# Gated delta rule of a two-block model: the chunk inverse in 64x64 products, value rows scaled by ScalarE, modulation steps placed elsewhere

## The chip, the cores and the metric

The kernel runs on one core of a Trainium2 chip. The metric is the device time of one execution in microseconds; of the kernel before there are three runs. The profile shows one more execution with its own time.

## The reference, cut to what matters

The program computes two transformer-like blocks over 256 tokens of width 2048. The part around the change is the gated delta rule of the first block: 8 heads, key and value width 128, chunks of 64 tokens in the reference. Each chunk solves a unit lower triangular system.

```python
def gated_delta_chunked(q, k, v, log_a, beta):
    qc, kc, vc = to_chunks(q), to_chunks(k), to_chunks(v)
    g = jnp.cumsum(...); bc = to_chunks(beta)
    gamma = jnp.exp(jnp.where(incl, g[..., :, None] - g[..., None, :], -jnp.inf))
    kk = jnp.einsum('nbhtk,nbhsk->nbhts', kc, kc)
    m = jnp.where(strict, bc[..., :, None] * kk * gamma, 0.0)
    a_mat = jnp.eye(CHUNK) + m
    rhs = jnp.concatenate([vc * bc[..., None], kc * (bc * jnp.exp(g))[..., None]], axis=-1)
    sol = lax.linalg.triangular_solve(a_mat, rhs, left_side=True, lower=True, unit_diagonal=True)
    u, w = sol[..., :DV], sol[..., DV:]
    def step(S, xs):
        v_new = u_c - w_c @ S
        o = qd_c @ S + qk_c @ v_new
        S = S * tl_c + kt_c^T @ v_new
        return S, o

mod = silu(c) @ w_ada + b_ada      # 12288 modulation values, used by the blocks
o = rmsnorm(o, norm_w) * silu(g_out)
```

## The kernel before, in words

The kernel takes chunks of 128 tokens: 8 heads in 2 chunks are 16 matrices of 128x128. `phase_gdn` handles them in four quads (n = 0 to 3) of four matrices; one PSUM bank holds a quad. It runs alone between the first block's input product and its output product: every engine enters it through a barrier and leaves it through one.

The inverse of I + M is built by doubling. `T` starts as the identity, `U` as its transpose. For block sizes L = 1, 2, 4 to 64, the off-diagonal L x L blocks are filled in. The first size is a masked copy of M itself (`L2297`, `L2299`). Each later level (`l` = 0 to 5, `inv_levels`) has for each quad: TensorE forms p = NT^T T (`("p", l, n)`), ScalarE copies it to `P1` (`L2111`), TensorE forms d = U^T P1 and its transpose dt = P1^T U, and VectorE copies both under a mask into `T` (`L2308`) and `U` (`L2311`) with `copy_predicated`. In the last level only dt and `U` are needed. All products go through `fill` (`L2144`), the transposes through `fill_turned` (`L2150`). A float32 product is two MATMUL instructions in the trace.

The order of work on each engine is the order in which its program is written; there is no scheduler. PSUM banks are taken in turn by `Banks`: six banks, the list `uses` fixes who gets which, and a bank is filled again only when the engine named in `uses` has emptied the use six places before.

VectorE also does work for later phases here, the modulation steps `ada.step` (`L273`, `L277`): `c` times a 128x512 piece of `w_ada`, added up. There are 48 of them (3 chunks of 16), and after each 16th step comes a fold (`L282`, `L288`, `L291`). Before the change, 6 steps stand ahead of the levels and the other 42 are spread over the 24 points (level, quad) of the levels. GpSimd issues the loads of these pieces (`L232`, 512 KB for two steps) into four slots; load q is issued once step 2q-7 is done and has to land before step 2q. GpSimd also makes the level masks in between.

Behind the levels, VectorE scales the value rows by beta (16 instructions, `L2334`) into `R`. Then follows a chain: vn0 = U^T R on TensorE, a copy by ScalarE, s, a copy, ks, a VectorE correction (`L2342`), vn1, a copy, the outputs o, their squares (`L2126`) and copy (`L2127`) by ScalarE, the row sums ss, logarithm and exponential, and two VectorE multiplications (`L2353`, `L2360`).

Of the kernel before, what the change touches and what calls it, by code (L numbers as in the profile page):

```python
# [14 lines left out]
P = 128  # L15
# [14 lines left out]
HH = 8  # L30
LEVELS = [64, 32, 16, 8, 4, 2, 1]
# [1427 lines left out]
GDN_CHUNKS, FRONT_STEPS = (15, 16, 17), 6  # L1459
# [541 lines left out]
def phase_gdn(nc, core, w_ada):  # L2001
# [23 lines left out]
    uses += [(("o", n), "act") for n in range(4)] + [(("ss", n), "act") for n in range(4)]  # L2025
    with ExitStack() as ctx:
# [6 lines left out]
            rs_ready, r1_ready, qkm_ready = (sem(n) for n in (  # L2033
                "silu_gg_ready", "eg_ready", "g1_ready", "g1_exp", "nt_ready", "tu_ready", "r0_ready",
                "eg_bc", "qd_ready", "sq_ready", "rs_ready", "r1_ready", "qkm_ready"))
# [6 lines left out]
        T, U, P1 = blocks(C0), blocks(C1), blocks(C2)  # L2042
        KTOK, QD = blocks(C3)[:, 0:HH, :], blocks(C3)[:, HH:2 * HH, :]
        R, VN = blocks(C0), blocks(C2)
        S = G1.rearrange("p (n t) -> p n t", t=P)[:, 0:HH, :]
        incl, strict = (ctx.enter_context(nc.sbuf_tensor(n, [P, P], F32)) for n in ("incl", "strict"))
        low_mask = ctx.enter_context(nc.sbuf_tensor("low_mask", [P, len(LEVELS), P], F32))
        ada = Ada(ctx, nc, core, [(w_ada, 0, chunk, 1) for chunk in GDN_CHUNKS], 1)
        steps, points = KT * len(GDN_CHUNKS) - FRONT_STEPS, 4 * NI
        block = ctx.enter_context(nc.Block())  # L2050
        quad = lambda a, n: a[:, 4 * n:4 * n + 4, :]
        quad_ps = lambda name: ps[:, banks.bank(name), :].rearrange("p (n t) -> p n t", t=P)
        as_blocks = lambda a: a.rearrange("p (n t) -> p n t", t=P)
# [4 lines left out]
        def _(pool):  # L2058
# [6 lines left out]
            for n in reversed(range(len(LEVELS))):  # L2065
                level_mask(nc, core, pool, low_mask, 1, n)
                made[n] = core.pool.n
                if n in (4, 2):
# [6 lines left out]
        def _(act):  # L2075
# [32 lines left out]
            for l in range(NI):  # L2108
                for n in range(4):
                    banks.wait_filled(act, ("p", l, n))  # L2110
                    nc.scalar.activation(quad(P1, n), quad_ps(("p", l, n)), ACT.Copy  # L2111
                                         ).then_inc(banks.emptied["act"], 1)
                if l == 0:
                    nc.scalar.activation(GB, GB, ACT.Exp).then_inc(eg_bc, 1)
# [8 lines left out]
            for n in range(4):  # L2123
# [3 lines left out]
                nc.scalar.activation(core.hT[:, HH + 2 * n:HH + 2 * n + 2, :], pso, ACT.Copy  # L2127
                                     ).then_inc(banks.emptied["act"], 1)
# [10 lines left out]
        def _(pe):  # L2139
# [35 lines left out]
            NTb = as_blocks(NT_)  # L2175
            for half in range(2):
# [1278 lines left out]
```

## Time and profile before

| what | value |
|---|---|
| median of 3 runs | 2905.76 us (2901.91 to 2911.55) |
| profiled execution, its own time | 2904.72 us |
| span of the profiled execution | 2903.0 us |
| mean granted TensorE clock | 0.970 |
| busy share of the span: PE, PEld, DVE, ACT, POOL | 95%, 87%, 71%, 47%, 16% |
| `phase_gdn` in the trace | from 560.9 to 696.5 us |

PE is TensorE's matrix instructions, PEld its weight loads, DVE VectorE, ACT ScalarE, POOL GpSimd. The time of an execution is a little longer than the span. Matrix instructions overlap, so that many of them back to back are read by the distance of their starts: a piece of x instructions with total length t and duration d of one has starts (t - d)/(x - 1) apart. The granted clock is a share of 2.4 GHz; 0.50 is the 1.2 GHz level.

### The profile page before, as it was taken

What the parts mean: (1) busy time and instruction counts of PE and PEld (TensorE: products, weight loads), DVE (VectorE), ACT (ScalarE), POOL (GpSimd) and SP (SyncE); (2) the same over time, 40 slices, a digit from 0 to 9 for tenths busy, and PEclk for the clock granted to TensorE, in tenths of its full rate; (3) what the DMA queues carried; (4) which work ended last, traced back from release to release, by engine and by line L of the source; (5) the groups of instructions that cost most, each with busy time, mean ns of one, the idle gap of its engine ahead of it and who ended that gap; (6) DMA issues with size and microseconds to landing.
All of it is one profiled execution on the core that took longest, in us unless ns stands there. A gap on an engine that the chain in (4) does not pass through costs nothing. (4 is left out here: it accounts for less than half of the span.)

```text
span 2903.0 us, 49916 instructions
## 1 busy us (share of the span) xinstructions
PE 2751.1 (95%) x19109; PEld 2538.8 (87%) x19109; DVE 2061.6 (71%) x2924; ACT 1374.0 (47%) x2210; POOL 457.4 (16%) x580
## 2 busy tenths in 40 slices
PE   8699999987989999999999999998989999999998
PEld 8689999886878888899998988887878888889998
DVE  6768996786787777787887678786577755555554
ACT  1354446534445555444544455455344444444454
POOL 1002998110011111111111021220011000000000
PEclk6799999998999999999999999999999999999999
DMA  9666666633657788788884666674568755555553
GB/s 386 237 209 241 216 218 197 211 105 130 237 196 273 270 276 277 259 279 282 264 280 134 175 232 221 204 239 135 186 218 279 243 189 186 180 189 166 176 190 129
DMA packets 290937, 632.43 MB, mean 218 GB/s; under 512 B 31490, under 2 KB 52422, under 8 KB 290502
## 3 DMA queue, kind: packets, MB, share of 16 engines
q1 hardware_dynamic: 239120, 484.78, 49.8%
q0 software_dynamic: 40192, 142.63, 14.6%
q10 hardware_dynamic: 11446, 2.54, 0.6%
q8 instruction: 123, 2.02, 0.3%
q14 instruction: 56, 0.46, 0.0%
HBM read 627.77 MB, written 2.10 MB: 217 GB/s over the span
## 5 line engine op out<-in xcount | busy, mean ns | idle before, releaser
L1187 DVE TENSOR_TENSOR weight_parts<-weights,weight_parts 128x1024 fp32r<-128x1024 f32 x584 | 706.9, 1222 | 295.7 <-ACT weight_parts L1108 294.6
L1108 ACT ACTIVATE weight_parts<-weights 128x1024 fp32r<-128x1024 f32 x584 | 607.2, 1057 | 557.0 <-PE accumulators L1297 240.4
L1286 PE MATMUL accumulators<-h_parts,weight_parts 128*128 128x512 f32 x2816 | 778.7, 398 | 20.6 <-DVE h_parts L1174 9.5
L1286 PEld LDWEIGHTS accumulators<-h_parts,weight_parts 128*128 128x128 f32 x2816 | 486.0, 190 | 90.5 <-DVE h_parts L1174 9.8
L1297 PEld LDWEIGHTS accumulators<-h_parts,weight_parts 128*128 128x128 f32 x2944 | 453.4, 190 | 71.0 <-DVE weight_parts L1187 10.5
L1297 PE MATMUL accumulators<-h_parts,weight_parts 128*128 128x256 f32 x2944 | 474.0, 283 | 6.8 <-DVE weight_parts L1187 6.5
L1332 PE MATMUL accumulators<-h_parts,weight_parts 128*128 128x256 f32 x1728 | 436.3, 284 | 1.8 <-DVE weight_parts L1187 1.8
L1334 PE MATMUL accumulators<-h_parts,weight_parts 128*128 128x256 f32 x1728 | 435.8, 284 | 0.0
L1332 PEld LDWEIGHTS accumulators<-h_parts,weight_parts 128*128 128x128 f32 x1728 | 334.1, 193 | 2.3 <-DVE weight_parts L1187 2.3
L1334 PEld LDWEIGHTS accumulators<-h_parts,weight_parts 128*128 128x128 f32 x1728 | 334.0, 193 | 0.0
L1328 PE MATMUL accumulators<-h_parts,weight_parts 128*128 128x256 f32 x1728 | 279.9, 285 | 8.9 <-ACT weight_parts L1108 8.9
L1652 PE MATMUL accumulators<-in_h_parts,in_weight_parts 128*128 128x256 f32 x1024 | 260.5, 287 | 22.9 <-DVE in_weight_parts L1973 22.8
L1654 PE MATMUL accumulators<-in_h_parts,in_weight_parts 128*128 128x256 f32 x1024 | 257.6, 284 | 0.0
L1812 ACT ACTIVATE in_weight_parts<-weights 128x512 fp32r<-128x512 f32 x256 | 157.2, 631 | 203.7 <-PE accumulators L1654 143.6
L1328 PEld LDWEIGHTS accumulators<-h_parts,weight_parts 128*128 128x128 f32 x1728 | 240.1, 193 | 9.3 <-ACT weight_parts L1108 9.3
L1973 DVE TENSOR_TENSOR in_weight_parts<-weights,in_weight_parts 128x512 fp32r<-128x512 f32 x256 | 187.6, 746 | 76.4 <-ACT in_weight_parts L1812 75.7
L2833 PE MATMUL accumulators<-in_h_parts,in_weight_parts 128*128 128x256 f32 x1632 | 216.9, 287 | 9.8 <-DVE in_weight_parts L3218 4.1
L2833 PEld LDWEIGHTS accumulators<-in_h_parts,in_weight_parts 128*128 128x128 f32 x1632 | 203.4, 192 | 21.1 <-issue 8.7
L1652 PEld LDWEIGHTS accumulators<-in_h_parts,in_weight_parts 128*128 128x128 f32 x1024 | 196.9, 192 | 27.6 <-DVE in_weight_parts L1973 27.3
L1654 PEld LDWEIGHTS accumulators<-in_h_parts,in_weight_parts 128*128 128x128 f32 x1024 | 197.2, 193 | 0.0
L2969 ACT ACTIVATE in_weight_parts<-weights 128x512 fp32r<-128x512 f32 (+6 forms) x224 | 120.9, 555 | 153.5 <-PE accumulators L2833 147.2
L3218 DVE TENSOR_TENSOR in_weight_parts<-weights,in_weight_parts 128x512 fp32r<-128x512 f32 (+6 forms) x224 | 129.7, 595 | 74.1 <-ACT in_weight_parts L2969 73.2
(404 smaller groups left out, 3497.3 us busy)
## 6 DMA issues: line engine op xcount, KB each, us to landing
weights<-in_w_ff SPq DMA_DIRECT2D x256, 512.0 KB, 5.4
weights<-in_w_in SPq DMA_DIRECT2D x160, 512.0 KB, 5.1
h_t<-in_ada_w POOLq DMA_DIRECT2D x96, 512.0 KB, 6.4
weights<-in_ffn_w_gate SPq DMA_DIRECT2D x88, 512.0 KB, 4.5
weights<-in_ffn_w_up SPq DMA_DIRECT2D x88, 512.0 KB, 4.6
weights<-in_ffn_w_down SPq DMA_DIRECT2D x88, 512.0 KB, 4.2
weights<-in_w_out SPq DMA_DIRECT2D x64, 512.0 KB, 4.7
wide<-in_ada_w POOLq DMA_DIRECT2D x128, 256.0 KB, 3.9
```

Of the source, the lines that this page charges most:

```text
L1108: nc.scalar.activation(w[:, held:held + take, 0, :], core.ring[:, q % RING, k:k + take, :], ACT.Copy).then_inc(core.high_ready, take)
L1187: ins = nc.vector.tensor_tensor(w[:, held:held + take, 1, :], core.ring[:, q % RING, k:k + take, :], w[:, held:held + take, 0, :].bitcast( ...
L1286: nc.tensor.matmul(core.ps[:, nt, :], high, x[:, kt].rearrange("p a t -> p (a t)"), start=(kt == 0), stop=False, skip_group_check=True)
L1297: ins = nc.tensor.matmul(rest(nt) if two else acc(c, nt), w[:, held, 1, nt * P:(nt + 1) * P], x[:, kt, 0, :], start=False, stop=(kt == KT ...
L1328: nc.tensor.matmul(accs[nt], w[:, held, 0, cols[nt]], xk[:, 0, :], start=(first and nt % 2 == 0), stop=False, skip_group_check=True)
L1332: nc.tensor.matmul(accs[nt], w[:, held, 0, cols[nt]], xk[:, 1, :], start=False, stop=False, skip_group_check=True)
L1334: ins = nc.tensor.matmul(accs[nt], w[:, held, 1, cols[nt]], xk[:, 0, :], start=False, stop=(last and nt % 2 == 1), skip_group_check=True)
L1652: nc.tensor.matmul(acc(c, nt), w[:, k, 0, nt * P:(nt + 1) * P], x[:, kt, 1, :], start=False, stop=False, skip_group_check=True)
L1654: ins = nc.tensor.matmul(acc(c, nt), w[:, k, 1, nt * P:(nt + 1) * P], x[:, kt, 0, :], start=False, stop=(kt == KT - 1 and nt % 2 == 1), sk ...
L1812: nc.scalar.activation(w[:, k, 0, :], core.ring[:, g % RING, part, :], ACT.Copy).then_inc(core.high_ready, 1)
L1973: ins = nc.vector.tensor_tensor(w[:, k, 1, :], core.ring[:, g % RING, part, :], w[:, k, 0, :].bitcast(F32), ALU.subtract)
L2833: ins = nc.tensor.matmul(out, stationary[:, a], moving[:, b], start=(kt == 0 and i == 0 and j == 0), stop=(kt == KT - 1 and i == 2 and j = ...
```

## The change

1. The inverse is built for the two diagonal 64x64 blocks of each 128x128 matrix alone (`EDGES`, `TOP`, `LOW`). A compact tile holds the upper block on partitions 0 to 63 and the lower one on 64 to 127, so a matrix takes 64 columns, not 128 (`squares`; `T`, `UD`, `P1`). Every product of levels 0 to 4 is two 64x64x64 products, one on the upper left and one on the lower right quarter of the array. d and dt of a quad share one bank. The turned M is now made by such products with the identity, not by transposes.
2. The masked copies touch only the columns that a level can change (`columns_of`): 128 elements in each partition in place of 512.
3. The last level only fills the block that couples both halves. `U` in full form is put together by plain copies: 8 for the diagonal blocks, 4 for the coupling block; GpSimd clears the rest. The 64-wide level mask is gone, compact masks are copied by GpSimd.
4. ScalarE scales the value rows in place, two after each p copy of levels 2 and 3; `R` is gone.
5. Modulation steps: none ahead of the levels, two at each of the 20 points of levels 0 to 4 (`LEVEL_STEPS`), five before the key correction, two behind it, the last one (with the fold) behind the output multiplications.
6. The output bank is read by VectorE itself (`L2353` of before), ScalarE's copy `L2127` is gone.

```diff
+LEVEL_STEPS = (2, 2, 2, 2, 2)
+STEPS_BEFORE_KEYS, STEPS_BEFORE_OUTPUTS = 5, 2
...
-        for n in range(4):
-            uses += [(("d", l, n), "dve")] if l < NI - 1 else []
-            uses += [(("dt", l, n), "dve")]
+        uses += [(("d", l, n), "dve") for n in range(4)]
...
+    squares = lambda a: flat(a, HH // 2).rearrange("p (n t) -> p n t", t=HP)
+    T, UD, P1 = squares(C0), squares(C0 + HH // 2), squares(C2)
+    U, VN = blocks(C1), blocks(C2)
...
 # GpSimd
+    for edge in EDGES:
+        copy(up_square[edge, 1:, :], core.up_mask[edge, 1:, edge])
...
+    for edge in EDGES:
+        copy(low_square[edge, n, :], low_mask[edge, n, edge])
+    if n == len(LEVELS) - 1:
+        nc.gpsimd.memset(U[LOW, :, TOP], 0.0).then_inc(cleared, 1)
...
 # ScalarE
-    nc.scalar.activation(quad(P1, n), quad_ps(("p", l, n)), ACT.Copy
+    nc.scalar.activation(quad(P1, n)[rows_of], half_ps(("p", l, n), 0)[rows_of], ACT.Copy
+    if l in (2, 3):
+        for h in (2 * n, 2 * n + 1):
+            nc.scalar.activation(value(l - 2, h), value(l - 2, h), ACT.Copy, scale=pc[:, l, h:h + 1])
...
-    nc.scalar.activation(core.hT[:, HH + 2 * n:HH + 2 * n + 2, :], pso, ACT.Copy)
...
 # TensorE
-    fill(("p", l, n), [(quad_ps(("p", l, n))[:, j, :], NTb[:, 4 * n + j, :], T[:, 4 * n + j, :], True, True)
-                       for j in range(4)])
+    fill(("p", l, n), [(p[e, j, :], NTb[e, m, e], T[e, m, :], True, True) for j, m in in_quad(n) for e in EDGES])
...
+    fill(("d", l, n), [(d[e, j, :], UD[e, m, :], P1[e, m, :], True, True) for j, m in in_quad(n) for e in EDGES]
+                    + [(dt[e, j, :], P1[e, m, :], UD[e, m, :], True, True) for j, m in in_quad(n) for e in EDGES])
...
 # VectorE
-    for step in range(4):
-        ada.step(dve, 0, step)
...
-    nc.vector.copy_predicated(quad(T, n), bcast(low_mask[:, m, :].bitcast(I32), 4), quad_ps(("d", l, n)))
...
+    nc.vector.copy_predicated(columns_of(quad(T, n), L, 0), mask_of(low_square, m, L, 0),
+                              columns_of(half_ps(("d", l, n), 0), L, 0))
+    nc.vector.copy_predicated(columns_of(quad(UD, n), L, 1), mask_of(up_square, m, L, 1),
+                              columns_of(half_ps(("d", l, n), 1), L, 1))
+    sum_steps(LEVEL_STEPS[l])
...
-    for c in range(2):
-        for h in range(HH):
-            ins = nc.vector.tensor_scalar(R[:, c * HH + h, :], big[:, GV + h, c * P:(c + 1) * P], ...)
+    for n in range(4):
+        for edge in EDGES:
+            nc.vector.tensor_copy(quad(U, n)[edge, :, edge], quad(UD, n)[edge])
+    for n in range(4):
+        nc.vector.tensor_copy(quad(U, n)[TOP, :, LOW], half_ps(("d", NI - 1, n), 1)[TOP])
+    sum_steps(STEPS_BEFORE_KEYS)
```

The order of TensorE's products in the levels, from the turned M on; first before (the rows of levels 2 to 4 read as those of level 1; `wide,gdn_work` are the p products, `wide` the others; of the 48 in level 0, 16 are the qk products):

```order
L2150 MATMUL accumulators<-ident,gdn_work 128x128 x8
L2150 MATMUL accumulators<-ident,wide 128x128 x16
L2144 MATMUL accumulators<-wide,gdn_work 128x128 x16
L2144 MATMUL accumulators<-wide 128x128 x48
L2144 MATMUL accumulators<-wide,gdn_work 128x128 x16
L2144 MATMUL accumulators<-wide 128x128 x32
```

and now, with line numbers of the changed file:

```order
L2164 MATMUL accumulators<-ident,gdn_work 64x64 x16
L2170 MATMUL accumulators<-ident,wide 128x128 x16
L2164 MATMUL accumulators<-wide,gdn_work 64x64 x32
L2164 MATMUL accumulators<-wide 64x64 x64
L2164 MATMUL accumulators<-wide 128x128 x16
L2164 MATMUL accumulators<-wide,gdn_work 64x64 x32
L2164 MATMUL accumulators<-wide 64x64 x64
```

Level 1 had 16 + 32 products of 128x128 and now has 32 + 64 of 64x64, twice as many.

VectorE around the end of the levels, before (the last two quads of level 5, then the value rows and the key correction):

```order
L2311 COPY_PREDICATED wide<-up_mask,accumulators 128x512
L277 SCALAR_TENSOR_TENSOR ada_sums<-ada_weights,c_act,ada_sums 128x512 x2
L2311 COPY_PREDICATED wide<-up_mask,accumulators 128x512
L277 SCALAR_TENSOR_TENSOR ada_sums<-ada_weights,c_act,ada_sums 128x512 x2
L282 TENSOR_TENSOR ada_sums<-ada_sums 128x512
L288 STREAM_TRANSPOSE ada_sums<-ada_sums 128x512
L291 TENSOR_REDUCE ada_rows<-ada_sums 128x16
L2334 TENSOR_SCALAR wide<-wide,gdn_token_cols 128x128 x16
L2342 SCALAR_TENSOR_TENSOR wide<-accumulators,gdn_token_cols,wide 128x128 x8
L2353 SCALAR_TENSOR_TENSOR h_t<-h_t,small_vectors,wide 128x512 x4
```

and now (the last quad of level 4 stands ahead):

```order
L2359 COPY_PREDICATED wide<-low_square,accumulators 128x4x32
L2361 COPY_PREDICATED wide<-up_square,accumulators 128x4x32
L278 SCALAR_TENSOR_TENSOR ada_sums<-ada_weights,c_act,ada_sums 128x512 x2
L2381 COPY wide<-wide 64x4x64 x8
L2384 COPY wide<-accumulators 64x4x64 x4
L278 SCALAR_TENSOR_TENSOR ada_sums<-ada_weights,c_act,ada_sums 128x512 x5
L2392 SCALAR_TENSOR_TENSOR wide<-accumulators,gdn_token_cols,wide 128x128 x8
L278 SCALAR_TENSOR_TENSOR ada_sums<-ada_weights,c_act,ada_sums 128x512 x2
L2404 SCALAR_TENSOR_TENSOR h_t<-accumulators,small_vectors,wide 128x512 x4
L278 SCALAR_TENSOR_TENSOR ada_sums<-ada_weights,c_act,ada_sums 128x512
```

The value rows are no longer ahead of the key correction, and the third fold, which stood before the chain of outputs, now stands inside it.

## Rows read from the trace of the kernel before

**Rows 1.** Windows of `phase_gdn`: length, busy per engine, PEclk (granted clock), DMA share, GB/s.

```profile
565.00:570.00 5.00, 5.00 (x18) 3.50 (x17) 2.63 (x5) 1.20 (x2) 4.53 (x10) 0.50 0.97 343
...
632.00:645.70 13.70, 10.65 (x96) 10.46 (x95) 11.66 (x19) 2.39 (x4) 2.90 (x4) 1.00 0.50 154
...
657.40:671.20 13.80, 2.56 (x23) 2.37 (x22) 12.87 (x30) 0.00 (x0) 0.00 (x0) 0.69 0.13 39
678.60:696.50 17.90, 14.05 (x103) 11.26 (x102) 7.88 (x17) 11.65 (x19) 0.00 (x0) 1.00 0.00 1
```

**Rows 2.** Groups by line in 560.9 to 696.5.

```profile
L2311 DVE COPY_PREDICATED wide<-up_mask,accumulators 128x512 f32<-128x512 int32 x24 | 17.3, 720 | 0.9 <-PE accumulators L2144 0.7
L2308 DVE COPY_PREDICATED wide<-low_mask,accumulators 128x512 f32<-128x512 int32 x20 | 14.5, 725 | 6.2 <-PE accumulators L2144 6.2
```

**Rows 3.** Timeline of DVE: start, length, instructions, idle before.

```profile
574.71 1.28 DVE L2259 TENSOR_TENSOR gdn_work<-accumulators,gdn_work 128x512 f32<-128x512 f32 x2
...
590.41 0.74 DVE L2308 COPY_PREDICATED wide<-low_mask,accumulators 128x512 f32<-128x512 int32 x1 [3.48 <-PE accumulators L2144]
...
594.31 1.41 DVE L277 SCALAR_TENSOR_TENSOR ada_sums<-ada_weights,c_act,ada_sums 128x512 f32<-128x512 f32 x2
595.64 0.72 DVE L2308 COPY_PREDICATED wide<-low_mask,accumulators 128x512 f32<-128x512 int32 x1
596.26 0.72 DVE L2311 COPY_PREDICATED wide<-up_mask,accumulators 128x512 f32<-128x512 int32 x1
...
601.62 2.48 DVE L2259 TENSOR_TENSOR gdn_work<-accumulators,gdn_work 128x512 f32<-128x512 f32 x4
```

**Rows 4.** Timeline of ACT at the front, and its scaling of 128x128 pieces.

```profile
572.12 1.05 ACT L2090 ACTIVATE gdn_work<-gdn_work 128x1024 f32<-128x1024 f32 x1
...
585.09 2.18 ACT L2105 ACTIVATE wide<-accumulators,gdn_token_cols 128x128 f32<-128x128 f32 x8
```

**Rows 5.** Timeline of PE.

```profile
563.37 3.38 PE L2144 MATMUL accumulators<-gates,pick 8*128 8x512 f32 x4
...
585.27 4.11 PE L2144 MATMUL accumulators<-wide,gdn_work 128*128 128x128 f32 x32
...
604.31 7.31 PE L2144 MATMUL accumulators<-wide 128*128 128x128 f32 x64
...
671.28 6.25 PE L2144 MATMUL accumulators<-wide 128*128 128x128 f32 x32 [11.32 <-issue]
```

**Rows 6.** Timeline of DVE in the levels and behind them.

```profile
610.85 0.69 DVE L282 TENSOR_TENSOR ada_sums<-ada_sums 128x512 f32<-128x512 f32 x1
...
618.05 2.29 DVE L2323 TENSOR_TENSOR gdn_work<-gdn_work,incl 128x2048 f32<-128x2048 f32 x1
...
630.90 1.22 DVE L2327 TENSOR_TENSOR wide<-wide,gdn_work 128x1024 f32<-128x1024 f32 x1
...
667.96 3.21 DVE L2334 TENSOR_SCALAR wide<-wide,gdn_token_cols 128x128 f32<-128x128 f32 x16
678.59 2.40 DVE L2342 SCALAR_TENSOR_TENSOR wide<-accumulators,gdn_token_cols,wide 128x128 f32<-128x128 f32 x8 [7.41 <-PE accumulators L2144]
```

**Rows 7.** Timeline of PE in other phases: parts of the array.

```profile
555.08 0.29 PE L190 MATMUL accumulators<-modulation,fold 128*32 128x28 f32 x8
...
1651.85 0.88 PE L2689 MATMUL accumulators<-wide,h_t 128*64 128x30 f32 x12
...
1707.60 0.93 PE L2763 MATMUL accumulators<-wide 64*128 64x128 f32 x8
```

**Rows 8.** The same two lines apart, ns min/median/max of one, with shapes.

```profile
L2689 PE MATMUL accumulators<-wide,h_t x128: 221/221/242, 1651.8 to 1676.8; 128*64 128x30 f32 x128
...
L2763 PE MATMUL accumulators<-wide x8: 272/374/378, 1707.6 to 1708.2; 64*128 64x128 f32 x4, 64*128 64x256 f32 x4
```

**Rows 9.** Loads of ada_weights in 560 to 700, 512 KB each.

```profile
DMA to landing us min/median/max: 3.8/4.0/6.7
```

**Rows 10.** Timeline of POOL: its seventh load, behind the first five masks.

```profile
575.35 0.73 POOL L232 DMA_DIRECT2D ada_weights<-in_w_ada  x1 [0.45 <-POOL low_mask L153]
```

More of the change, by code:

```diff
@@ L30 @@
 HH = 8
+HP = P // 2
 LEVELS = [64, 32, 16, 8, 4, 2, 1]
@@ L2024, in phase_gdn @@
     uses += [(("ks", n), "dve") for n in range(2)] + [(("vn1", n), "act") for n in range(2)]
-    uses += [(("o", n), "act") for n in range(4)] + [(("ss", n), "act") for n in range(4)]
+    uses += [(("o", n), "dve") for n in range(4)] + [(("ss", n), "act") for n in range(4)]
     with ExitStack() as ctx:
@@ L2047, in phase_gdn @@
         low_mask = ctx.enter_context(nc.sbuf_tensor("low_mask", [P, len(LEVELS), P], F32))
+        low_square, up_square = (ctx.enter_context(nc.sbuf_tensor(n, [P, len(LEVELS), HP], F32)) for n in (
+            "low_square", "up_square"))
+        ident_square = ctx.enter_context(nc.sbuf_tensor("ident_square", [P, HP], F32))
         ada = Ada(ctx, nc, core, [(w_ada, 0, chunk, 1) for chunk in GDN_CHUNKS], 1)
-        steps, points = KT * len(GDN_CHUNKS) - FRONT_STEPS, 4 * NI
         block = ctx.enter_context(nc.Block())
@@ L2052, in phase_gdn @@
         quad_ps = lambda name: ps[:, banks.bank(name), :].rearrange("p (n t) -> p n t", t=P)
+        half_ps = lambda name, n: quad(ps[:, banks.bank(name), :].rearrange("p (n t) -> p n t", t=HP), n)
+        EDGES = (slice(0, HP), slice(HP, P))
+        TOP, LOW = EDGES
         as_blocks = lambda a: a.rearrange("p (n t) -> p n t", t=P)
@@ L2175, in _, with in_quad @@
             NTb = as_blocks(NT_)
+            def in_quad(n):
+                return [(j, 4 * n + j) for j in range(4)]
             for half in range(2):
@@ L2185, in _ @@
                 for n in range(4):
-                    pe.wait_ge(tu_ready, 4 * l + n + 1)
-                    fill(("p", l, n), [(quad_ps(("p", l, n))[:, j, :], NTb[:, 4 * n + j, :], T[:, 4 * n + j, :],
-                                        True, True) for j in range(4)])
+                    if l == 0:
+                        pe.wait_ge(tu_ready, n + 1)
+                    else:
+                        pe.wait_ge(banks.emptied["dve"], n_dve[("d", l - 1, n)])
+                    p = half_ps(("p", l, n), 0)
@@ L2196, in _ @@
                 if l == 0:
                     fill_products("qk", q_all, 0, 4)
-            pe.wait_ge(tu_ready, 4 * NI + 4)
-            pe.wait_ge(r0_ready, 1)
+            pe.wait_ge(r0_ready, 2 * HH)
             for n in range(2):
-                fill(("vn0", n), [(quad_ps(("vn0", n))[:, j, :], U[:, 2 * (4 * n + j), :], R[:, 4 * n + j, :],
+                pe.wait_ge(banks.emptied["dve"], n_dve[("d", NI - 1, 2 * n + 1)])
+                fill(("vn0", n), [(quad_ps(("vn0", n))[:, j, :], U[:, 2 * (4 * n + j), :], value(0, 4 * n + j),
@@ L2213, in _ @@
                 fill(("vn1", n), [(quad_ps(("vn1", n))[:, j, :], U[:, 2 * (4 * n + j) + 1, :],
-                                   R[:, HH + 4 * n + j, :], True, True) for j in range(4)])
+                                   value(1, 4 * n + j), True, True) for j in range(4)])
             pe.wait_ge(qd_ready, 1)
@@ L2286, in _ @@
             distances(4, 5)
-            ada.step(dve, 0, 4)
-            ada.step(dve, 0, 5)
             strict_products(0, masked)
@@ L2341, in _ @@
                     h = 4 * n + j
-                    ins = nc.vector.scalar_tensor_tensor(out=R[:, HH + h, :], in0=quad_ps(("ks", n))[:, j, :],
-                                                         scalar=pc[:, 6, h:h + 1], in1=R[:, HH + h, :],
+                    ins = nc.vector.scalar_tensor_tensor(out=value(1, h), in0=quad_ps(("ks", n))[:, j, :],
+                                                         scalar=pc[:, 6, h:h + 1], in1=value(1, h),
                                                          op0=ALU.mult, op1=ALU.add)
```

112 lines of the change are left out of this document (68 added, 44 removed).

## The prediction

> **What bounds the kernel now.** Over the span TensorE is the busy engine, but the change lies inside one closed phase, so I read that stretch alone, 560.9 to 696.5 us. Engines enter and leave it together, so what it gets shorter the whole gets shorter, unless the next phase starts worse. First the windows: in the levels VectorE is busy 11.7 of 13.7 us and TensorE 10.7 of 13.7, at full clock, so both are near a bound [rows 1]. From 657.4 to 671.2 VectorE works 12.9 of 13.8 us and TensorE 2.6; the clock falls. Then the groups: VectorE waited for TensorE only 6.2 and 0.7 us at the 44 level copies [rows 2]. Then both timelines: a step and a copy follow each other without a gap [rows 3], and TensorE waits 11.3 us until the value rows are scaled, at 671.28 [rows 5]. So from 590.4 to 671.3 VectorE sets the pace, with TensorE close behind it. From 671.3 on it is a chain of small products and copies (7.3 us to the key correction at 678.59 [rows 5, 6], then 17.9 us to the end [rows 1]) on which nobody is busy long.
>
> **The front.** First level copy of VectorE before: 590.41 [rows 3]. Taking away six steps lets VectorE start earlier, but the products of K and K wait for the exponential that ScalarE ends at 572.12 + 1.05 = 573.2 [rows 4], and VectorE took them at 574.71 [rows 3]. So of six steps (4 us) only about 1.3 us comes off. TensorE then turns M in 64 instructions where 16 stood; at the price found below, 0.03 us, that is 1.9 us against 1.8 (16 x 0.114). The p products of level 0 take 64 x 0.03 = 1.9 us where 32 took 3.7: 1.8 off. Together 590.4 - 1.3 - 1.8 = 587.3; I take 588.0, since with a bank per quad for d and dt and the qk products between, the first quads run in a tight ring of six banks. Bounds: 587 to 592 (all of these products at 0.06).
>
> **TensorE's price, the main unknown.** 128x128 instructions start 7.31/64 = 0.114 us apart [rows 5]. No row shows 64x64 products on the two diagonal quarters. The nearest with 64 columns of the array is L2689: with 0.22 as the length of one, (0.88 - 0.22)/11 = 0.060 us apart [rows 7, 8]. Whether two of them overlap: L2763 uses 64 rows of the array, alternating between the upper and the lower half, and its 8 instructions (four of 128 columns, four of 256) start (0.93 - 0.38)/7 = 0.079 apart [rows 7, 8], below the 0.114 that 128 columns alone would take. L190 uses four groups of 32 columns: 8 end within 0.29 us of the first start, so they are at most 0.036 apart. Both parts of the array work side by side, by rows and by columns. I take 0.030 (two at 0.060); bounds 0.030 and 0.060, and 0.12 at the 1.2 GHz level. A level has 64 + 128 = 192 instructions, hence 5.8 us where 96 took 10.9. In the Trainium skill, TensorEngine Tiling (Array Packing), section Restrictions and Gotchas, it says that different row tiles cannot access the same PSUM bank at once. L2763 writes two banks and L190 one bank with one row tile, so no run here shows the case of this change, in which both quarters write one bank at different partitions. By that rule a level takes 192 x 0.060 = 11.5 us, which is the first rival.
>
> **VectorE in levels 0 to 4.** A copy of 128x512 starts the next after 0.62 [rows 3]. The new ones have 128 elements in four-dimensional patterns. Nearest rows: 128x128 out of SBUF, 3.21/16 = 0.20 apart; out of PSUM with a scalar column, 2.40/8 = 0.30 apart [rows 6]. I take 0.25, with 0.20 and 0.32 as bounds. A step costs 0.667 (two to 595.64 - 594.31 = 1.33 [rows 3]).
> - 5 levels x 8 copies x 0.25 = 10.0
> - 40 steps x 0.667 = 26.7
> - two folds, each three operations of 0.7 [rows 6]: 4.2
> - qk 2.5 [rows 3], its mask 2.3, QD 1.2 [rows 6]: 6.0
> - one wait for TensorE after level 0, as the third and fourth p of level 1 need the banks that qk leaves: 0.7
>
> Sum 47.6, so the levels end at 635.6. Before they ran from 590.4 to 667.96, 77.5 us. The rest of the 30 us is the last level's 4 copies, one fold and the six steps moved elsewhere. A plain period is 8 x 0.25 + 8 x 0.667 = 7.3 us for VectorE. The loop through TensorE is about as long: last copy at 6.0, p of the last quad 0.5, d of the first 1.0, latencies 0.3, in all 7.8. The mask, QD and the folds cover this in levels 1 to 3, so I charge nothing.
>
> **Putting U together.** 8 copies of 64x256 at 0.25 and two of the four from PSUM at 0.3 stand before the first product of the chain: 2.6 us where the value rows took 3.2 [rows 6]. The last level's products (32 instructions on one quarter, 0.06 each, 1.9 us) run beside the steps of level 4. vn0 then starts at 638.3, against 671.28. Scaling the value rows costs ScalarE 16 x 0.27 = 4.3 us (2.18 for 8 [rows 4]) over two levels, in which it works 2.4 of 13.7 us [rows 1]: hidden. If it were not, it would come late to p by 0.5 us a quad.
>
> **The chain behind.** vn0 to the key correction 7.3 us, and 17.9 to the end, as before: TensorE again stands idle before vn0, so I leave the clock at what it was (32 instructions from 671.28 took 6.25 us [rows 5], 0.20 each, the 1.2 GHz level). The five steps (3.3 us) fit inside the 7.3 (DVE idle for 7.41 [rows 6]); two more and one fold stand where VectorE waited for outputs and roots, and ScalarE's four copies of 0.6 were beside TensorE's products. 638.3 + 7.3 + 17.9 = 663.5, so 33.0 us off.
>
> **Cover that may go.** Weights: a load now has three points, 5.5 us, plus a copy pair, 6.0, for issue 0.73 and landing 4.0 [rows 9, 10]; the rate needed is 512 KB in 1.83 us, 286 GB/s, and 343 has been seen [rows 1]. GpSimd's added copies (two for a mask, one clearing) stand before masks that were ready at 575.35 [rows 10] and are needed after 581; 10 short operations at up to 0.9 fit. Clock: TensorE will be busy 5.8 of some 8 to 11 us, on half its cells. From 565 to 570 it was busy throughout, on and behind products with 8 rows, and was granted 0.50 [rows 1, 5]. One period without extra VectorE work and at 1.2 GHz costs 11.5 + 0.3 - 7.8 = 4 us. I charge 2 us for half a level of it.
>
> Sum: -33.0 + 2 = -31. The profiled execution took 2904.7, so 2873.7; the median before is 1.1 above that one, so 2874.8, rounded 2875.
>
> **Rivals.**
> 1. The quarters take turns, or the clock stays at 1.2 GHz through the levels: 0.060 per instruction. TensorE sets the pace: p from 584.5 on, 5 x 11.5 + qk 3.6 + last level 1.9 = 647.6, U 1.4, then 25.2: 674.2, -22, 2884. For: no row has this shape. Against: L190, L2763 [rows 7, 8]. 0.12.
> 2. The loads set the pace: several under way, landing at 6.7 as the slowest did [rows 9], (6.7 + 0.7 - 0.5)/3 = 2.3 us a point, +0.47 at 20 points: -31 + 9 = -22, 2884. Against: breaks of 2 us and more let the loads catch up. 0.07.
> 3. Slower: the quarters take turns and the clock is at 1.2 GHz, 0.12 each. From 587: 5 x 192 x 0.12 = 115, qk 6.8, last level 3.8, to 712.8; with 0.6 + 25.2 the end is 738.6, +42, 2948. It decides from (671.3 - 0.6 - 584.5 - 3.6)/(960 + 32) = 0.083 us per instruction on. Before, TensorE kept full clock in the levels [rows 1] with whole-array products; half of that work could be read as too little. 0.04.
> 4. The phase gets shorter but nothing is gained, because the output phase then waits for weights: its first 8 loads were issued before the phase and nothing of it hangs on the phase's length. 0.03.
>
> My forecast has the remaining 0.74. Its own range is 2867 to 2883 (copies 0.20 to 0.32 at 52 places, clock 0 to 8 us). Rivals 1 and 2 end at 2884, so 2864 to 2889 holds a little over 8 in 10. A change under 0.3% (9 us) can't be told from none: faster 0.93, same 0.03, slower 0.04.
>
> **What would show it.** Right: p and d instructions in pairs a few ns apart, 0.03 on average; level copies 0.25 apart; vn0 some 33 us earlier than at 671.3; TensorE still with gaps in the levels; no DVE wait for ada_weights. Rival 1: DVE waits for `L2164` 4 us a level and TensorE has no gap. Rival 2: DVE waits for DMA. Wrong also if the chain from vn0 to the end is not 25 us, say because the third fold comes late for the last sums.

## The result, and the profile after

The changed kernel took 2868.59 us (median of 4 runs, 2862.77 to 2874.77) against 2903.84 us for the kernel before (4 runs, 2901.82 to 2911.55): ratio 0.9875, 95% interval 0.9854 to 0.9896. The forecast was 2875, range 2864 to 2889. The profiled execution of the changed kernel took 2862.77 us, its span was 2861.0 against 2903.0, so 42.0 less.

Where the 42 us lie is read from four marks in both traces: VectorE's first instruction of the phase, its first level copy, the first product of vn0, the first key correction.

| stretch | before | forecast | after |
|---|---|---|---|
| start of the phase | 560.95 | | 556.43 |
| front, to the first level copy | 29.46 | 27.0 | 26.33 |
| levels and putting U together, to vn0 | 80.87 | 50.3 + 2 for the clock | 48.12 |
| vn0 to the key correction | 7.31 | 7.3 | 6.57 |
| key correction to the end | 17.94 | 17.9 | 17.93 |
| phase | 135.58 | 104.6 | 98.95 |

The phase gave 36.6 us (forecast 31). Another 4.5 us were there before it began, though the program ahead of it is the same. They lie in one place: VectorE waits there for a load of `w_ada`, first before, then after:

```profile
112.52 0.49 DVE L273 TENSOR_SCALAR attn_t<-scaled,c_act 128x512 f32<-128x512 f32 x1 [10.63 <-DMA scaled<-in_w_ada]
```

```profile
107.53 0.49 DVE L274 TENSOR_SCALAR attn_t<-scaled,c_act 128x512 f32<-128x512 f32 x1 [5.31 <-DMA scaled<-in_w_ada]
```

This wait is 10.6 us in the profiles of all four kernels of the old kind (the kernel before and the three experiments on it) and 4.5 to 5.3 us in all eight with the changed one, and the phase starts at 561.0 to 565.5 in the four and at 555.0 to 560.5 in the eight. The experiment with the steps in the gaps has the short wait, and the three on the kernel before that ran on the same chip have the long one. So it goes with the changed kernel and not with chance or the chip. Nobody forecast it, no run tests it, and why the load lands earlier stays open. Behind the phase come 2202.0 to 2212.5 us in the twelve profiles, without a trend. The medians are 35 us apart, which holds the phase, this wait and what executions differ in: the changed kernel, profiled a second time, had the same phase to 0.04 us and a span of 2867.8 where the first had 2861.0.

Windows of the changed phase (columns as in [rows 1]; the first answers to the first row there, the next two to the second, the last to the last; the fourth runs from vn0 to the key correction):

```profile
565.00:570.00 5.00, 5.00 (x14) 2.55 (x14) 1.80 (x5) 2.83 (x5) 3.85 (x11) 0.84 0.06 25
...
605.00:610.00 5.00, 2.85 (x57) 2.39 (x54) 5.00 (x13) 2.88 (x9) 2.17 (x3) 0.71 0.48 120
612.00:618.50 6.50, 5.79 (x166) 5.65 (x164) 6.31 (x16) 1.15 (x3) 2.17 (x3) 0.85 0.73 234
...
630.90:637.50 6.60, 6.60 (x43) 6.60 (x44) 3.99 (x8) 2.39 (x4) 0.00 (x0) 0.73 0.15 58
637.50:655.50 18.00, 14.14 (x104) 11.28 (x102) 12.03 (x23) 9.80 (x15) 0.00 (x0) 1.00 0.01 1
```

From 605 to 610 VectorE is still full (5.00 of 5.00) and TensorE has gaps (2.85 of 5.00). The stretch of 13.8 us with VectorE at work and TensorE at 2.6 [rows 1] is gone: from 630.9 on both work.

The groups that answer to [rows 2], and the first block size out of SBUF:

```profile
L2361 DVE COPY_PREDICATED wide<-up_square,accumulators 128x128 f32<-128x128 int32 x20 | 6.6, 328 | 0.0
L2359 DVE COPY_PREDICATED wide<-low_square,accumulators 128x128 f32<-128x128 int32 x20 | 6.4, 318 | 3.4 <-PE accumulators L2164 3.4
...
L2342 DVE COPY_PREDICATED wide<-up_square,gdn_work 64x128 f32<-64x128 int32 x8 | 3.7, 463 | 0.1
```

31.8 us of level copies became 13.0, and VectorE waits 3.4 us for TensorE where it waited 6.9 (2.06 of the 3.4 before the first level copy). The mean lengths say little here, because copies overlap: what counts on VectorE is the distance of starts, as its timeline shows (it answers to [rows 3, 6]):

```profile
582.76 0.45 DVE L2359 COPY_PREDICATED wide<-low_square,accumulators 128x128 f32<-128x128 int32 x1 [2.06 <-PE accumulators L2164]
583.01 0.49 DVE L2361 COPY_PREDICATED wide<-up_square,accumulators 128x128 f32<-128x128 int32 x1
...
592.80 0.30 DVE L2359 COPY_PREDICATED wide<-low_square,accumulators 128x128 f32<-128x128 int32 x1 [0.80 <-PE accumulators L2164]
593.01 0.29 DVE L2361 COPY_PREDICATED wide<-up_square,accumulators 128x128 f32<-128x128 int32 x1
593.21 1.41 DVE L278 SCALAR_TENSOR_TENSOR ada_sums<-ada_weights,c_act,ada_sums 128x512 f32<-128x512 f32 x2
...
627.61 2.40 DVE L2381 COPY wide<-wide 64x256 f32<-64x256 f32 x8
630.03 1.41 DVE L2384 COPY wide<-accumulators 64x256 f32<-64x256 f32 x4
631.47 3.40 DVE L278 SCALAR_TENSOR_TENSOR ada_sums<-ada_weights,c_act,ada_sums 128x512 f32<-128x512 f32 x5
637.45 2.40 DVE L2392 SCALAR_TENSOR_TENSOR wide<-accumulators,gdn_token_cols,wide 128x128 f32<-128x128 f32 x8 [2.58 <-PE accumulators L2164]
```

Level copies are 0.20 us apart, 0.23 to 0.29 in level 0, where they take two elements and leave two. TensorE's timeline (it answers to [rows 5]; "8\*128" counts the rows and columns of the array):

```profile
565.77 3.88 PE L2164 MATMUL accumulators<-gates,pick 8*128 8x512 f32 x8
...
591.55 3.95 PE L2164 MATMUL accumulators<-wide 64*64 64x64 f32 x128
...
604.62 0.68 PE L2164 MATMUL accumulators<-wide,gdn_work 64*64 64x64 f32 x16 [1.70 <-DVE wide L2361]
...
610.15 5.63 PE L2164 MATMUL accumulators<-wide 64*64 64x64 f32 x128
...
630.88 5.57 PE L2164 MATMUL accumulators<-wide 128*128 128x128 f32 x32 [1.20 <-issue]
```

The 128 products of a level start (3.95 - 0.24)/127 = 0.029 us apart, and TensorE waits for VectorE's copies, 1.70 us at 604.62. From 599 on the single starts come in pairs, 0.006 to 0.007 us apart, with 0.052 us to the next pair. The 5.63 us at 610.15 are the same 128 with the clock partly at 0.50.

### The profile page after: what moved, and what is told of

Read it like the earlier page. It is cut to its first block and busy times, and to the rows that moved or that the text cites. A ratio compares the mean times of both kernels' runs of the same rounds, so it can differ in the third digit from the quotient of the medians.

```text
span 2861.0 us, 50952 instructions
## 1 busy us (share of the span) xinstructions
PE 2726.7 (95%) x19637; PEld 2514.4 (88%) x19637; DVE 2038.9 (71%) x2921; ACT 1369.9 (48%) x2222; POOL 462.9 (16%) x592
## 5 line engine op out<-in xcount | busy, mean ns | idle before, releaser
L1655 PE MATMUL accumulators<-in_h_parts,in_weight_parts 128*128 128x256 f32 x1024 | 263.2, 289 | 13.9 <-DVE in_weight_parts L1976 13.6
L1657 PE MATMUL accumulators<-in_h_parts,in_weight_parts 128*128 128x256 f32 x1024 | 260.0, 286 | 0.0
L2884 PE MATMUL accumulators<-in_h_parts,in_weight_parts 128*128 128x256 f32 x1632 | 216.8, 287 | 9.7 <-DVE in_weight_parts L3269 4.1
L1648 PE MATMUL accumulators<-in_h_parts,in_weight_parts 128*128 128x256 f32 x1024 | 177.0, 296 | 3.7 <-DVE in_h_parts L1846 3.7
```

The costliest lines, as they stand in the source:

```text
L1648: nc.tensor.matmul(acc(c, nt), w[:, k, 0, nt * P:(nt + 1) * P], x[:, kt, 0, :], start=(kt == 0 and nt % 2 == 0), stop=False, skip_group_ch ...
L1655: nc.tensor.matmul(acc(c, nt), w[:, k, 0, nt * P:(nt + 1) * P], x[:, kt, 1, :], start=False, stop=False, skip_group_check=True)
L1657: ins = nc.tensor.matmul(acc(c, nt), w[:, k, 1, nt * P:(nt + 1) * P], x[:, kt, 0, :], start=False, stop=(kt == KT - 1 and nt % 2 == 1), sk ...
L2884: ins = nc.tensor.matmul(out, stationary[:, a], moving[:, b], start=(kt == 0 and i == 0 and j == 0), stop=(kt == KT - 1 and i == 2 and j = ...
```

## The experiments

Sections in us as in the table above, from one profile each; "ratio" is of the medians, against the kernel before, run beside each. A median moves with more than the phase, so that what a part is worth is read from the phase, and the median stands beside it.

| kernel | median | ratio, 95% | front | levels | vn0 to keys |
|---|---|---|---|---|---|
| one quarter | 2878.3 | 0.9891 (0.9867 to 0.9915) | 28.65 | 59.23 | 6.50 |
| quarters apart | 2869.81 | 0.9856 (0.9824 to 0.9888) | 30.66 | 49.98 | 6.46 |
| whole squares | 2871.52 | 0.9865 (0.9839 to 0.989) | 28.64 | 53.07 | 6.58 |
| small steps | 2850.49 | 0.9805 (0.9782 to 0.9828) | 28.64 | 35.29 | 4.93 |
| before + value rows | 2897.51 | 0.9965 (0.995 to 0.998) | 30.29 | 75.59 | 7.65 |
| before + half columns | 2898.84 | 0.9975 (0.9963 to 0.9987) | 29.31 | 72.80 | 7.67 |
| before + steps moved | 2902.36 | 0.9978 (0.9966 to 0.9991) | 28.02 | 76.96 | 6.41 |
| steps in the gaps | 2859.58 | 0.9835 (0.9819 to 0.9851) | 28.62 | 44.60 | 5.24 |
| changed, again | 2869.21 | 0.9859 (0.9843 to 0.9876) | 26.34 | 48.14 | 6.50 |
| first size | 2855.44 | 0.982 (0.98 to 0.9839) | 32.10 | 41.91 | 6.37 |

The last part of the phase was 17.9 us in all of them.

**All products on one quarter.**

```diff
-    for j, m in in_quad(n) for e in EDGES
+    for j, m in in_quad(n) for e in (TOP, TOP)
```

> The changed kernel, but every p, d and dt product of levels 0 to 4 that belonged to the lower right quarter of the array repeats the one of the upper left quarter instead (the lower blocks of the inverse are not computed); as many instructions, all in one quarter. Theory: the two quarters overlap, and the gain needs it. Alone in one quarter an instruction costs 0.060 us, a level 192 x 0.060 = 11.5 us of TensorE, and the five levels take 61 us in place of 44.9: 14 to 18 us slower than the changed kernel (2869), so about 2885. Rival A: VectorE sets the pace and the overlap is of no use: within 3 us of the changed kernel. Rival B: the clock falls as well, 0.12 us per instruction: over 60 us slower than the changed kernel.

TensorE's timeline and windows of this kernel:

```profile
602.07 7.63 PE L2164 MATMUL accumulators<-wide 64*64 64x64 f32 x128
609.53 3.89 PE L2164 MATMUL accumulators<-wide,gdn_work 64*64 64x64 f32 x64
613.27 7.63 PE L2164 MATMUL accumulators<-wide 64*64 64x64 f32 x128
```

```profile
609.00:620.00 11.00, 11.00 (x192) 11.00 (x191) 10.71 (x21) 3.76 (x12) 2.86 (x4) 1.00 0.62 197
620.00:631.00 11.00, 11.00 (x192) 11.00 (x190) 8.17 (x18) 3.76 (x12) 2.69 (x5) 1.00 0.59 184
```

On one quarter the products are (7.63 - 0.22)/127 = 0.058 us apart, twice the 0.029 of two quarters, and a level takes 11.2 us with TensorE busy throughout. VectorE's wait before the level copies grows from 3.4 to 14.8 us and the levels get 11.1 us longer, the whole phase 13.4. So the quarters do work side by side, though they write one bank, and the change needs it. The median is 9.7 us above that of the changed kernel, less than the 14 to 18 expected: the levels and U took 59.2 us where 61 stood for the levels alone. A quarter of the array, busy without gaps, kept the granted clock at 1.00.

**The two quarters in turn instead of in pairs.**

```diff
-    for j, m in in_quad(n) for e in EDGES
+    for e in EDGES for j, m in in_quad(n)
```

> The changed kernel, but within each quad first the four products of the upper left quarter, then the four of the lower right one (8 instructions of one quarter behind each other), for p, d and dt. Theory: the quarters have queues of their own that are filled ahead, so the overlap stays: within 2 us of the changed kernel. Rival: only neighbours overlap; then it is as with one quarter, 14 to 18 us slower.

TensorE's timeline of this kernel:

```profile
600.60 4.59 PE L2164 MATMUL accumulators<-wide 64*64 64x64 f32 x122
```

(4.59 - 0.22)/121 = 0.036 apart: most of the overlap stays although eight instructions of one quarter stand in a row. Of the 127 distances between the single starts of one such level, 48 are 0.004 to 0.006 us and the others 0.052 to 0.059, so instructions of both quarters still start together. The levels are 1.9 us longer, the median 1.2 us, within the interval, as expected. The queues that the theory speaks of are not shown by any row.

**Level copies over whole squares.** 256 elements where the change has 128; `columns_of` and `mask_of` are left out of both copies.

> The changed kernel, but the 40 masked copies of levels 0 to 4 run over all 64 columns of a square (256 elements) and not over the half that can change (128). Theory: VectorE sets the pace of the levels, so each copy's 128 / 0.96 GHz = 0.133 us shows: 40 x 0.133 = 5.3, 4 to 6 us slower than the changed kernel. Rival: the loop through TensorE sets it: under 1.5 us slower.

VectorE's copies of this kernel:

```profile
597.00 0.45 DVE L2359 COPY_PREDICATED wide<-low_square,accumulators 128x256 f32<-128x256 int32 x1
597.33 0.44 DVE L2361 COPY_PREDICATED wide<-up_square,accumulators 128x256 f32<-128x256 int32 x1
```

They are 0.33 us apart in place of 0.20. Levels 53.07, +4.95 for 40 copies, 0.12 each: VectorE's time reaches the end of the levels in full. The median is only 2.9 us above that of the changed kernel, under the 4 to 6 expected, and the intervals overlap, so that the total doesn't show it.

**Small steps.**

```diff
+        n = 8 if getattr(self, "small", False) and q < 20 else CW
...
+        if small:
+            acc, w = acc[:, 0:8], w[:, 0:8]
```

> The changed kernel, but the 40 modulation steps in the levels work on 8 columns in place of 512 (the first two of each chunk are a clearing of 512 columns), and their 20 loads bring 8 columns: most of three modulation chunks is left out. Theory: VectorE paces the levels now, with TensorE's loop close behind (last copy, p of quad 3, d of quad 0: about 6 us a level with nothing else on VectorE), so of the 26.7 us of steps only 9 to 13 come off: about 2857. Rival A: VectorE alone counts: 22 to 27 us off. Rival B: TensorE already paces the levels: under 3 us off.

Levels 35.29, -12.8. VectorE's waits of this kernel (waiting instruction, releaser, total, times, longest):

```profile
DVE wide L2364 <- PE accumulators L2169: 3.4, 7, 2.2
DVE wide L2364 <- POOL low_mask L154: 2.3, 1, 2.3
```

Windows from the first level copy to the first copy of U, the changed kernel and this one:

```profile
582.76:627.61 44.85, 36.36 (x940) 34.59 (x936) 43.30 (x92) 17.69 (x40) 19.83 (x34) 0.92 0.64 206
```

```profile
585.91:617.64 31.73, 30.93 (x911) 30.14 (x908) 27.00 (x93) 16.38 (x37) 17.04 (x34) 1.00 0.10 11
```

About 17 us of VectorE work are gone (34 steps at 0.14 in place of 0.66), and 12.8 came off the levels, within the 9 to 13 expected. What bounds them now is TensorE, busy 30.93 of 31.73 us. It had the full clock throughout, against a mean of 0.92 in the changed kernel, so a part of the 12.8 may be the clock's; how much isn't shown. The median is 18.1 us under that of the changed kernel, further than the 2857 expected; the profiled phase is 12.1 us shorter.

**The kernel before with the value rows on ScalarE alone.**

```diff
+    for h in (2 * n, 2 * n + 1):
+        nc.scalar.activation(value(l - 2, h), value(l - 2, h), ACT.Copy, scale=pc[:, l, h:h + 1])
...
-            ins = nc.vector.tensor_scalar(R[:, c * HH + h, :], big[:, GV + h, c * P:(c + 1) * P], ...)
```

> The kernel before with one part of the change alone: ScalarE scales the value rows in place, two after each p copy of levels 2 and 3, and VectorE's 16 instructions are gone. Theory (VectorE paces the levels and the value rows stand on its path, ScalarE has room): vn0 about 3.2 us earlier, since 3.21 us of VectorE work leave the path and nothing takes their place: levels 77.7 in place of 80.9, total about -3 us. Rival (the scaling comes late to p, 0.5 us a quad at 8 points, and TensorE sets the pace there): half of the gain or less is left, levels 79 to 81, total -1 to 0.

Levels -5.28, more than the 3.2 expected. VectorE's timeline of this kernel, and TensorE's:

```profile
668.70 0.72 DVE L2318 COPY_PREDICATED wide<-up_mask,accumulators 128x512 f32<-128x512 int32 x1
669.63 1.42 DVE L277 SCALAR_TENSOR_TENSOR ada_sums<-ada_weights,c_act,ada_sums 128x512 f32<-128x512 f32 x2 [0.21 <-DVE wide L2318]
671.08 0.69 DVE L282 TENSOR_TENSOR ada_sums<-ada_sums 128x512 f32<-128x512 f32 x1
```

```profile
648.12 8.94 PE L2151 MATMUL accumulators<-wide 128*128 128x128 f32 x64
...
669.53 5.70 PE L2151 MATMUL accumulators<-wide 128*128 128x128 f32 x25 [4.37 <-DVEq L2321]
```

vn0 starts on the last copy, and the last point's two steps and the fold (3.4 us) are now beside it; before they stood ahead of the value rows. With the 3.2 of the value rows that makes 6.6; a stretch of products at the lower clock (8.94 for 64, 7.31 in [rows 5]) would take 1.6 back, which leaves 5.0. The phase is 4.1 us shorter. The median moved by 10.3 where 3 was expected; where the rest lies isn't shown (the profiled execution was the slowest of six).

**The kernel before with half columns.**

```diff
-    copy_predicated(quad(T, n), bcast(low_mask[:, m, :]), quad_ps(("d", l, n)))
+    copy_predicated(columns_of(quad(T, n), L, 0), mask_of(low_mask, m, L, 0), columns_of(quad_ps(("d", l, n)), L, 0))
...
```

> The kernel before with the masked copies of the levels limited to the columns that a level can change: 256 elements in place of 512, products still 128x128 over the whole array. Theory (VectorE sets the pace and TensorE stands close behind it): a copy goes from 0.62 to about 0.35 us apart, 44 of them give 12 us on VectorE, but TensorE's 10.9 us a level with about 1 us of turnaround then becomes the bound, so the levels fall from 80.9 to about 73 to 76 and VectorE's waits for TensorE grow from 7 to 11 us or more. Rival (the 64x64 products are of no use, VectorE's copies give all): levels 69 to 70, with VectorE's waits unchanged.

Windows of this kernel, 12 us each (a level has 96 products):

```profile
618.00:630.00 12.00, 12.00 (x108) 12.00 (x109) 11.32 (x19) 2.59 (x6) 2.72 (x5) 1.00 0.53 146
...
642.00:654.00 12.00, 12.00 (x110) 12.00 (x109) 8.38 (x16) 2.95 (x5) 2.88 (x4) 1.00 0.51 139
```

TensorE is full, with products (12 us for 108) 0.111 us apart, 10.7 us a level. Levels 72.80, -8.1, just under the 73 to 76 expected, with VectorE's waits at 8.7 us and not at 11 or more; the median moved by 9.0. The rival fell. Cheaper copies alone end at TensorE's price of a level. That the 64x64 products let the rest through is the difference to the changed kernel; no run has them with copies of 512 elements.

**The kernel before with the steps moved alone.** None ahead, 40 at the 24 points, 5, 2 and 1 behind.

> The kernel before with the modulation steps alone moved: none ahead of the levels, 40 spread over the 24 points of the levels, five behind the value rows, two ahead of the output multiplications, the last with its fold behind them. Theory (VectorE paces front and levels, the chain has room): front 1.3 us shorter, levels 1.3 (two steps) + 2.1 (the third fold) shorter, behind them nothing longer: total -4.7 us. Rival 1 (what VectorE gives up in front is not on the path, only what leaves the levels counts): -3.4. Rival 2 (the third fold comes late for the last sums): the part behind the key correction grows by 1 us or more over 17.9.

Front -1.44, levels -3.9, vn0 to keys -0.9: 6.3 in the phase. The median moved by 5.4, against 4.7 expected. Rival 2 fell (the last part took 17.9); against rival 1 speaks the front's 1.44, though three fronts with the same steps (the kernel before, value rows, half columns) differ by 1.0 among themselves.

**The steps in the gaps** (on the changed kernel).

```diff
-LEVEL_STEPS = (2, 2, 2, 2, 2)
-STEPS_BEFORE_KEYS, STEPS_BEFORE_OUTPUTS = 5, 2
+LEVEL_STEPS = (2, 1, 2, 1)      # by quad
+STEPS_AT_FRONT, STEPS_BEFORE_LEVELS, STEPS_BEFORE_KEYS, STEPS_BEFORE_OUTPUTS = 5, 3, 7, 2
```

> The changed kernel with its 48 modulation steps moved again, to where its trace shows VectorE waiting: five ahead of the distances of row 4 (it waits 3.25 us there for ScalarE), three ahead of the first level copy (2.06 us for TensorE), 30 in the levels (2, 1, 2, 1 per level in place of 2, 2, 2, 2), seven before the key correction (2.58 us of waiting beside the five that are there), two ahead of the outputs, one behind. Theory (VectorE sets the pace of the changed levels and TensorE's loop has about 1.3 us of room a level): levels 10 x 0.667 = 6.7 us shorter, 41.5 in place of 48.1, front and chain as they are: about -6 us against the changed kernel. Rival (TensorE and its latencies bound a level by now): levels 45 to 47, -1 to -3 us, with VectorE's waits in the levels grown by as much as the steps that left.

VectorE's timeline of this kernel, and its window from the first level copy to the first copy of U:

```profile
563.53 2.07 DVE L278 SCALAR_TENSOR_TENSOR ada_sums<-ada_weights,c_act,ada_sums 128x512 f32<-128x512 f32 x3
566.30 0.52 DVE L2284 TENSOR_SCALAR gdn_work<-gdn_work,gdn_token_cols 128x128 f32<-128x128 f32 x2 [0.70 <-ACT gdn_work L2099]
...
620.45 0.30 DVE L2361 COPY_PREDICATED wide<-low_square,accumulators 128x128 f32<-128x128 int32 x1 [1.50 <-PE accumulators L2164]
```

```profile
583.61:624.94 41.33, 34.82 (x919) 33.72 (x916) 37.58 (x82) 16.87 (x38) 13.00 (x20) 0.92 0.63 193
```

Levels 44.60, 3.5 shorter, between both theories. The ten steps that left them were 6.1 us and not 6.7, since two of them are of the cheap kind (0.40). Somewhat over half reached the end; VectorE's idle time in the window rose from 1.55 (44.85 - 43.30) to 3.75, most of it in waits for TensorE. The eight steps in front cost nothing that shows: its 28.62 is what the two other kernels with the same products and the lower clock in front have (28.64). Because of that slower front the phase is only 2.6 us shorter. The median is 9.0 us under that of the changed kernel's first runs and 9.6 under that of its second; the intervals of the ratios lie apart by a hair for the first and overlap for the second, so about -6 is neither shown nor refuted.

**The changed kernel again, and the first size from the accumulators.**

```diff
+    + [(half_ps(("nt", n), 1)[e, j, :], core.ident[e, e], NTb[e, m, e], True, True) ...]
-    for edge in EDGES: copy_predicated(... quad(NTb, n)[edge, :, edge] ...)
+    copy_predicated(columns_of(quad(UD, n), 1, 1), mask_of(up_square, last, 1, 1), columns_of(half_ps(("nt", n), 1), 1, 1))
```

> The changed kernel once more, word for word, to stand beside the next one on the same chip. The front of its first profile was 26.3 us, that of four kernels with the same front 28.6 to 30.7, with the granted clock at 0.50 for a longer time. Theory (where the clock falls to 1.2 GHz in the front varies from execution to execution): the front comes out near 28.6 here, levels 48, behind them 6.6 + 17.9. Rival (something in the other kernels makes their fronts longer): 26.3 again.

> The version with the steps in the gaps, and the first block size of UD read from the accumulators: TensorE multiplies M by the identity a second time from the other side (64 more 64x64 products, 128 instructions, 3.8 us by 0.03 each at full clock), and VectorE takes UD in one copy of 128 partitions and 128 elements per quad in place of two of 64 partitions out of SBUF. Theory (the strided copy out of SBUF is what is slow, 0.47 us each, and these copies stand on the path to the first p): VectorE's eight copies of 3.8 us become four of 0.25, so -2.8 us on it; TensorE's added products lie partly beside the transposes of the values: front and levels together 2 to 3 us less than the 73.2 of the version with steps in the gaps. Rival (TensorE at the half clock sets this place): 0 to -1 us, and VectorE waits for TensorE before the first copies. Against the changed kernel of the same call both together should give -8 to -13 us.

The changed kernel repeated its front to 0.01 us: 26.34. The theory of a front that varies from execution to execution fell in this one repeat. What the fronts of 26.3 and 28.6 us differ in is one group. TensorE's timeline of the kernel with whole squares, whose front has the same instructions, against 3.88 at 565.77 above:

```profile
564.54 7.19 PE L2164 MATMUL accumulators<-gates,pick 8*128 8x512 f32 x8
```

These eight products of 8 rows run at 0.50 in one kernel and mostly at 1.00 in the other. In the twelve traces they take 3.8 to 4.3 us seven times (the kernel before among them) and 7.19 five times (quarters apart, whole squares, small steps, steps in the gaps, first size). The front with one quarter is long for its own reason: its p products are twice as far apart. Why the clock comes back at 566 in one kernel and not in another stays open, and so do the further 2 us in the front of the quarters apart.

The kernel with the first size from the accumulators had the slower form: front 32.10. Its timeline of VectorE:

```profile
583.47 0.44 DVE L2350 COPY_PREDICATED wide<-low_square,accumulators 128x128 f32<-128x128 int32 x1
583.72 0.48 DVE L2352 COPY_PREDICATED wide<-up_square,accumulators 128x128 f32<-128x128 int32 x1
...
586.40 0.45 DVE L2350 COPY_PREDICATED wide<-low_square,accumulators 128x128 f32<-128x128 int32 x1 [1.36 <-PE accumulators L2164]
...
592.65 0.45 DVE L2360 COPY_PREDICATED wide<-low_square,accumulators 128x128 f32<-128x128 int32 x1 [2.73 <-PE accumulators L2164]
```

The copy out of the accumulators costs about 0.30 where two out of SBUF took 0.95, but VectorE now waits 1.36 and 2.73 us for TensorE, as the rival said; front and levels are 74.0 against 73.2. In this profile the first size gives nothing: the phase is 98.3 us, against 96.4 with the steps in the gaps and 98.9 of the changed kernel. The median is below those of the other complete kernels all the same: 2855.44, 13.8 us under the changed kernel beside it (0.982 against 0.9859, intervals apart), just over the 8 to 13 expected. The profiled phases account for 0.6 us of that. It beats both kernels; where it gains, and that the first size has a part in it, isn't shown.

## Why the prediction was right

**What bounded the kernel.** VectorE did, with TensorE just behind: half columns alone end with TensorE busy 12.00 of 12.00 us. The three parts that could be put into the kernel before shorten the phase by 4.1 (value rows), 7.9 (half columns) and 6.3 (steps), 18.3 together; the change gave 36.6. That the other half is the 64x64 products and the narrower copies that they allow is a subtraction: no run adds the parts up. What a run does show is that without the overlap of the quarters 13.4 of the 36.6 us are gone.

**What was luck.** The forecast of 31 stood for the phase, which gave 36.6, and for the whole, which by the medians gave 35. In the whole lie also some 5 us from the load ahead of the phase, which no term covered. And the prediction's own range doesn't follow from the terms it names: 52 copies 0.05 cheaper and 2 us of clock take 4.6 off 2875, hence 2870; 52 copies 0.07 dearer and 6 us more of clock give 2885; written were 2867 and 2883. The measured 2868.59 lies under 2870 and inside the wide range of 2864 to 2889.

**The front.** Right: 29.46 - 1.3 - 1.8 = 26.4, measured 26.33 (VectorE took the products of K and K 1.5 us earlier in the phase). The 0.7 added for a ring of six banks was not there. The steps alone gave 1.44 where 1.3 was reckoned. That holds for the changed kernel in both its profiles; its relatives with the lower clock in front had 28.6, which the prediction has no term for.

**TensorE's price.** 0.030 was taken, 0.029 measured, with the pairs that the prediction asked for, and 0.058 on one quarter against 0.060. The bounds from L2689, L2763 and L190 [rows 7, 8] held. The rule in the Trainium skill, TensorEngine Tiling (Array Packing), section Restrictions and Gotchas, that different row tiles can't access one PSUM bank at once, is not what the trace shows here: the quarters at rows 0 and 64 write one bank, on different partitions, and run at half the distance of one quarter. Rival 1 is out. Its price was right, though: one quarter gave 11.2 us a level against 11.5.

**The levels.** 50.3 with U, measured 48.1. The copies are 0.20 us apart in four of five levels, not 0.25 (1.5 us less in all). The first two steps of each of the three chunks are plain multiplications, 0.40 us apart and not 0.667 (1.6 less). Waits inside the levels were 1.3 where 0.7 stood. So the levels ended after 44.9 us, not 47.6; U then took 3.3 to vn0, at 0.30 us per copy and not 0.25, where the prediction reckons 2.6 and puts 2.7 into its sum.

**The clock.** It did fall in the levels, from 607 to 614, after TensorE had been busy only 2.28 of 5.00 us. Windows of the changed kernel ahead of the fall and in it:

```profile
602.00:607.00 5.00, 2.28 (x64) 1.87 (x60) 5.00 (x10) 1.43 (x5) 0.72 (x1) 1.00 0.38 120
...
607.00:614.00 7.00, 5.87 (x106) 5.69 (x108) 6.46 (x15) 2.42 (x8) 2.17 (x3) 0.51 0.84 265
```

d took 5.63 us for 3.95, but VectorE had its steps and QD to do meanwhile and waited only 0.54 us for it, a wait that the levels' 1.3 already hold. So the 2 us charged were not lost, the largest single miss. Together: 0.7 (front) + 2.7 (levels) - 0.6 (U) + 2 (clock) + 0.7 (vn0 to keys) = 5.5, the difference between 31 and 36.6.

**The chain.** vn0 to the keys took 6.57 us, since part of it ran at full clock (0.73 in its window); in the version with steps in the gaps, whose vn0 had the full clock, 5.24. The end took 17.93 of 17.9, so the third fold was not late. Scaling the value rows was hidden, 0.68 us for two against 2.18 for eight [rows 4]; ScalarE's timeline of the changed kernel, p copy and scaling:

```profile
605.35 0.38 ACT L2127 ACTIVATE wide<-accumulators 128x256 f32<-128x256 f32 x1 [5.15 <-PE accumulators L2164]
605.62 0.68 ACT L2133 ACTIVATE wide<-wide,gdn_token_cols 128x128 f32<-128x128 f32 x2
```

**The other rivals.** Rival 2: VectorE never waited for ada_weights in the changed phase. Rival 3: at 0.029 us far from 0.083. Rival 4: the part behind the phase took 2205.6 us in the first profile and 2212.5 in the second, 2206.5 before, so no gain of this size was lost there.

## What to carry to other kernels

A small block-diagonal product can take both diagonal quarters of the array at once. Here that took TensorE's work of a level from 10.9 to about 5.6 us (192 x 0.029). When two engines are close to each other, cutting the work of one stops at the other: half the columns in the copies gave 8 us of the levels alone, and TensorE was full. Filler work that leaves the path of the engine that sets the pace may bring only a part of its length, since the other engine is next; in the one case tried, 3.5 of 6.1 us. Look also at what stands between the last useful copy and the next product: here two steps and a fold of a later phase cost 3.4 us there, as much as scaling the value rows.

And compare what lies outside the changed phase too, over several profiles: a wait of 10.6 us had become one of 5 us 450 us ahead of the change.

## What the hardware showed that was not expected

- A copy_predicated of 64 partitions x 128 elements, every second one, out of SBUF took 0.48 to 0.50 us to the start of the next; one of 128 x 128 out of PSUM 0.22 to 0.30 where it takes one or two elements and leaves as many, and 0.20 where it takes four or more at a time.
- A single 64x64 quarter, busy without gaps, kept the granted clock at 1.00 for three levels, while products of 8 rows, also busy without gaps, had mostly 1.00 in seven traces and 0.50 in five (3.8 to 4.3 against 7.19 us for eight).
- Eight instructions of one quarter followed by eight of the other still came 0.036 us apart, many of them in pairs 0.004 to 0.006 us apart.
